# Up units of a SwiGLU block with seven half-block products in place of eight

## The reference

```
x = layer_norm(ALPHA * x + m @ lw['w_o'], lw['ln1_g'], lw['ln1_b'])
gate, up = jnp.split(x @ lw['w_up'], 2, axis=-1)          # w_up: 1024 x 5632
x = layer_norm(ALPHA * x + (jax.nn.silu(gate) * up) @ lw['w_down'], lw['ln2_g'], lw['ln2_b'])
```

## Time and profile before

| what | value |
|---|---|
| median of three executions | 2097.69 us |
| span of the profiled execution, first to last instruction | 2097.1 us |
| TensorE, matmul busy | 2072.3 us (99%) |
| VectorE busy | 1169.4 us (56%) |
| ScalarE busy | 713.2 us (34%) |
| GpSimd busy | 81.3 us (4%) |
| matmuls | 16020 |

### The profile page before, as it was taken

How to read it: one execution, slowest core, us unless ns; L and a number is a source line. 1 busy time by engine, 2 the same in 40 slices (tenths; PEclk the granted TensorE clock), 3 DMA queues, 4 the chain that set the end, 5 groups by cost and what they waited for, 6 DMA issues and landing times.

```text
span 2097.1 us, 38539 instructions
## 1 busy us (share of the span) xinstructions
PE 2072.3 (99%) x16020; PEld 1996.6 (95%) x16020; DVE 1169.4 (56%) x1886; ACT 713.2 (34%) x1152; POOL 81.3 (4%) x96
## 2 busy tenths in 40 slices
PE   7999999999999999999999999999999999999999
PEld 6899999898999999999998999989889999999998
DVE  5434645774377666654465365466724866566433
ACT  4232134444343232222343221354433433222232
POOL 1000000000011000000010000010000200000110
PEclk9999999999999999999999999999999999999999
DMA  5232222321132223223333222132213223323331
GB/s 171 78 77 58 61 54 64 93 62 51 51 101 81 85 85 90 83 81 93 86 92 83 78 59 76 40 93 59 63 34 93 84 81 90 90 80 88 84 90 54
DMA packets 287876, 163.45 MB, mean 78 GB/s; under 512 B 8984, under 2 KB 279552, under 8 KB 287744
## 3 DMA queue, kind: packets, MB, share of 16 engines
q1 hardware_dynamic: 283712, 152.07, 25.9%
q0 software_dynamic: 3552, 8.36, 1.3%
q10 hardware_dynamic: 480, 1.13, 0.2%
HBM read 156.86 MB, written 4.66 MB: 77 GB/s over the span
## 4 chain that ended last, share of the span: by engine, by line
PE 97%; DVE 1%; ACT 1%; issue 0%; DMA 0%; DVEq 0%; ACTq 0%
PE acc L696 50%; PE acc L682 27%; PE ring L718 4%; PE ring L802 2%; PE ring L956 2%; PE ring L975 1%; PE acc L718 1%; PE ring L964 1%; PE ring L1026 1%; PE ring L1008 1%; PE ring L1256 1%; PE ring L853 0%; PE ring L839 0%; PE ring L829 0%; PE ring L832 0%; PE acc L845 0%
## 5 line engine op out<-in xcount | busy, mean ns | idle before, releaser
L1388 ACT ACTIVATE whi<-raw 128x1024 fp32r<-128x1024 f32 (+6 forms) x340 | 312.0, 918 | 739.2 <-PE acc L696 404.0
L1970 DVE TENSOR_TENSOR wlo<-raw,whi 128x1024 fp32r<-128x1024 f32 (+6 forms) x340 | 355.0, 1046 | 299.7 <-ACT whi L1388 298.8
L696 PE MATMUL acc<-xh,whi 128*128 128x272 f32 x1376 | 310.7, 307 | 3.6 <-DVE xl L1970 3.4
L682 PE MATMUL acc<-xh,whi 128*128 128x274 f32 x1472 | 308.5, 290 | 0.0
L682 PE MATMUL acc<-xh,wlo 128*128 128x274 f32 x1472 | 305.9, 289 | 0.0
L682 PE MATMUL acc<-xl,whi 128*128 128x274 f32 x1472 | 305.5, 289 | 0.0
L696 PE MATMUL acc<-xh,wlo 128*128 128x272 f32 x1376 | 285.9, 289 | 0.0
L696 PE MATMUL acc<-xl,whi 128*128 128x272 f32 x1376 | 285.7, 289 | 0.0
L696 PEld LDWEIGHTS acc<-xh,whi 128*128 128x128 f32 x1376 | 218.2, 190 | 19.1 <-issue 14.4
L682 PEld LDWEIGHTS acc<-xh,whi 128*128 128x128 f32 x1472 | 232.2, 189 | 0.6
L682 PEld LDWEIGHTS acc<-xl,whi 128*128 128x128 f32 x1472 | 231.6, 189 | 0.0
(11 more groups left out here) (411 smaller groups left out, 3118.2 us busy)
## 6 DMA issues: line engine op xcount, KB each, us to landing
raw<-in_w_in_dram SPq DMA_DIRECT2D x104, 512.0 KB, 3.7
raw<-in_w_up_dram SPq DMA_DIRECT2D x88, 512.0 KB, 3.7
raw<-in_w_down_dram SPq DMA_DIRECT2D x32, 512.0 KB, 3.8
raw<-in_w_o_dram SPq DMA_DIRECT2D x16, 512.0 KB, 3.8
raw<-in_w_down_dram SPq DMA_DIRECT2D x16, 384.0 KB, 3.3
...
```

The lines of the kernel that those rows point to most:

```text
L682: last = pe.matmul(dst[:, at_:at_ + x1 - x0], wq[:, k * P:(k + 1) * P], x[:, k, x0:x1], start=k == 0 and q == 0, stop=k == KD - 1 and q == 2)
L696: last = pe.matmul(dst[:, b * 512:b * 512 + HALF], w[:, c:c + P], x[:, k0 + a, b * HALF:(b + 1) * HALF], start=start and a == 0 and q == 0 ...
L1388: return act.activation(dst, src, ACT.Copy)
L1970: return dve.tensor_tensor(out, a, b, op)
```

## The change

For the hidden blocks f = 4 to 21 (18 of 22, named **pairs**, p = 0 to 17), the product of x (two halves of the tokens by two halves of the depth) with the weights of both units (two halves of the depth by gate and up) is formed as a 2x2 by 2x2 block product with seven block products in place of eight, by the scheme of Strassen and Winograd. One block product is 4 k-blocks x 3 passes x 272 columns: 12 matmuls. Before, the same block took 8 k-blocks x 3 passes x 2 halves x 2 units = 96 matmuls; now it takes 84.

- **Activations.** The scheme takes x normalised. VectorE's `x_norm` and ScalarE's `x_gained` now do this within the first eight units, and VectorE makes four sums of blocks of x (`block_sums`, 128x1088 each). The seven blocks are split into high and low parts (`block_hi`, `block_lo`). `times_rstd` and `less_mean` leave the down stage; ScalarE only multiplies by ALPHA there.
- **Weights.** For each pair GpSimd makes four sums of quarters of the weights in three instructions (`weight_sum`: one 128x1024, two 128x512). Seven blocks of 128x512 are split by ScalarE (`weight_hi`) and VectorE (`weight_lo`), six products ahead of TensorE, into eight slots that reuse `whi`, `wlo`, and the space of `xh`/`xl`.
- **Results.** Products 0, 2, 4 and 6 of a pair add up in one bank of PSUM, 1 and 5 in a second, 3 in a third. Four intermediate values are copied out by ScalarE (`keep`), before TensorE adds the next product to the same bank. VectorE joins them (`pair_lin`), ScalarE takes the sigmoid, VectorE multiplies (`pair_h`).
- **Hidden values.** They stay unsplit in `hid` until the last pair, where ScalarE and VectorE split all 22 blocks, two at a time (`h_hi`, `h_lo`, 128x1088 each, 11 of each).
- The hardware loops of the up stage are gone; all is written out.

The diff, cut to what the prediction speaks of:

```diff
+STD_F = 4
+PAIRS = KF - STD_F
+SLOTS, AHEAD = 8, 6
+U_PAIRS = U_UP + 2 * STD_F
+
+PRODUCTS = ("x11_w11", "s3_t3", "s2_t2", "x12_w21", "s1_t1", "x22_t4", "s4_w22")
+OF_PAIR = len(PRODUCTS)
...
+                if 0 <= p < PAIRS:
+                    sp.wait_ge(*at("wt_lo", l, OF_PAIR * (p + 1)))
+                    passed(sp, "sp")
+                return not 0 <= p < PAIRS
...
+            for i, dst in enumerate((a, b, a, c, a, b, a)):
+                q = OF_PAIR * p + i
+                pe.wait_ge(*at("wt_lo", layer, q + 1))
+                if p == 0:
+                    pe.wait_ge(*at("xb_lo", layer, i + 1))
+                if p > 1 and i == 0:
+                    pe.wait_ge(*at("pr_h", layer, 2 * (p - 2) + 1))
+                elif p > 1 and i == 1:
+                    pe.wait_ge(*at("pr_lin", layer, 3 * (p - 2) + 3))
+                elif p > 1 and i == 3:
+                    pe.wait_ge(*at("pr_lin", layer, 3 * (p - 2) + 1))
+                elif i in (2, 4, 5, 6):
+                    pe.wait_ge(*at("pr_kept", layer, 4 * p + {2: 1, 4: 3, 5: 2, 6: 4}[i]))
+                w1, w2 = weight_slot(q)
+                first = i in (0, 1, 3)
+                for k in range(4):
+                    for r, (w, part) in enumerate(((w1, 0), (w1, 1), (w2, 0))):
+                        last = pe.matmul(dst[:, 0:HALF], w[:, k * P:(k + 1) * P], block_of(i, part)[:, k, :],
+                                         start=first and k == 0 and r == 0, stop=k == 3 and r == 2, skip_group_check=True)
+                last.then_inc(*inc("pr_done"))
...
+            if name in WEIGHT_TERMS:
+                act.wait_ge(*at("wt_sum", l, 3 * p + WEIGHT_TERMS[name]))
+            else:
+                loaded(l, U_PAIRS + 2 * p + (i == OF_PAIR - 1))
+            if q < SLOTS:
+                act.wait_ge(*used_unit(l, U_PAIRS - 2 if q < 2 else U_PAIRS - 1))
+            else:
+                act.wait_ge(*at("pr_done", l, q - SLOTS + 1))
+            copy(weight_slot(q)[0], weight_block(q)).then_inc(*inc("wt_hi"))
...
+            i = (0, 1, 2, 4)[n]
+            act.wait_ge(*at("pr_done", l, OF_PAIR * p + i + 1))
+            if p > 0:
+                act.wait_ge(*at("pr_lin", l, 3 * (p - 1) + (1, 2, 3, 2)[n]))
+            banks = pair_banks(p)
+            copy(kept[n], banks[1 if n == 1 else 0][:, 0:HALF]).then_inc(*inc("pr_kept"))
...
+            tail = {1: [(h_hi, 0), (h_hi, 2)], 2: [(h_hi, 4), (next_hi, U_DN)], 3: [(h_hi, 6)], 4: [(h_hi, 8), (h_hi, 10), (next_hi, U_DN + 1)],
+                    5: [(h_hi, 12)], 6: [(h_hi, 14), (h_hi, 16), (h_hi, 18), (h_hi, 20)]}
+            for p in range(PAIRS):
+                for i in range(OF_PAIR):
+                    if i in (0, 1, 2, 4):
+                        keep(l, p, (0, 1, 2, 4).index(i))
+                    if p == 0 and i == 0:
+                        act.sem_inc(*inc_by("w_hi", 2 * PAIRS))
+                        act.sem_inc(*inc_by("w_used", 2 * PAIRS))
+                    q = OF_PAIR * p + i + AHEAD
+                    if q < OF_PAIR * PAIRS:
+                        weight_hi(l, q)
...
+            def x_norm(l, k):
+                tt(y[:, k:k + 2, :], y[:, k:k + 2, :], rs[:, :].unsqueeze(1).broadcast_to([P, 2, T]), ALU.mult).then_inc(inc("x_prod", 2)[0], 2)
+                dve.wait_ge(*at("x_prod", l, k + 2))
+                tt(y[:, k:k + 2, :], y[:, k:k + 2, :], tmp[:, :].unsqueeze(1).broadcast_to([P, 2, T]), ALU.add).then_inc(inc("x_norm", 2)[0], 2)
...
+            def weight_lo(l, q):
+                dve.wait_ge(*at("wt_hi", l, q + 1))
+                hi, lo = weight_slot(q)
+                tt(lo, weight_block(q), f32(hi), ALU.subtract).then_inc(*inc("wt_lo"))
...
+                dve.wait_ge(*at("pr_sig", l, p + 1))
+                tt(gs[:, 0, :], gs[:, 0, :], gs[:, 1, :], ALU.mult).then_inc(*inc("pr_gate"))
+                dve.wait_ge(*at("pr_gate", l, p + 1))
+                dve.wait_ge(*at("pr_done", l, OF_PAIR * (p + 1)))
+                tt(hid[:, f, 0:HALF], gs[:, 0, 0:HALF], pair_banks(p)[0][:, 0:HALF], ALU.mult).then_inc(*inc("pr_h"))
+                tt(hid[:, f, HALF:T], gs[:, 0, HALF:T], hid[:, f, HALF:T], ALU.mult).then_inc(*inc("pr_h"))
...
+            x_steps = {1: [(x_norm, 0), (x_norm, 2)], 2: [(x_norm, 4)], 3: [(x_norm, 6)], 4: [(block_sums, B_S3), (block_sums, B_S1)],
+                       5: [(block_sums, B_S2), (block_sums, B_S4), (block_lo, 0)], 6: [(block_lo, 1), (block_lo, 2)],
+                       7: [(block_lo, 3), (block_lo, 4)]}
...
+            for q in range(2, AHEAD):
+                weight_lo(l, q)
+                if q < 4:
+                    block_lo(l, q + 3)
+            dve.sem_inc(*inc_by("w_lo", 2 * PAIRS))
+            tail = {1: [(h_lo, 0), (h_lo, 2)], 2: [(h_lo, 4)], 3: [(next_lo, U_DN), (h_lo, 6)], 4: [(h_lo, 8), (h_lo, 10)],
+                    5: [(h_lo, 12), (next_lo, U_DN + 1)], 6: [(h_lo, 14), (h_lo, 16), (h_lo, 18), (h_lo, 20)]}
+            for p in range(PAIRS):
+                for i in range(OF_PAIR):
+                    if i in (3, 4, 5):
+                        pair_lin(l, p, i - 3)
+                    if i == 6:
+                        pair_h(l, p)
+                    q = OF_PAIR * p + i + AHEAD
+                    if q < OF_PAIR * PAIRS:
+                        weight_lo(l, q)
+                    else:
+                        for step, n in tail[i]:
+                            step(l, n)
...
+                    pool.wait_ge(*at("wt_lo", l, OF_PAIR * p - 1))
+                pool.tensor_tensor(two(t13), later, earlier, ALU.subtract).then_inc(*inc("wt_sum"))
+            elif n == 1:
+                pool.wait_ge(*at("wt_sum", l, 3 * p + 1))
+                pool.tensor_tensor(t2, t13[:, 512:1024], w11, ALU.add).then_inc(*inc("wt_sum"))
+            else:
+                pool.wait_ge(*at("wt_sum", l, 3 * p + 2))
+                pool.tensor_tensor(t4, w21, t2, ALU.subtract).then_inc(*inc("wt_sum"))
```

283 lines of the change are left out of this document (211 added, 72 removed).

## The result

The changed kernel takes 2104.57 us (median of seven runs, 2100.29 to 2108.72), the kernel before 2097.69 us (seven runs, 2095.34 to 2098.98). The ratio is 1.0035, with an interval of 1.0025 to 1.0046: slower by a third of a per cent. I had forecast 2093 us. The time lies in the range of 2073 to 2110, but on the other side of no change, and above the 2084 to 2101 of my own case.

The account below looks back on a forecast made before the run. TensorE's matmuls were taken to bound the kernel. Per layer 28.8 - 14.1 - 4.8 - 7.6 = 2.3 us gained, 4.6 in all: span 2097.1 becomes 2092.5, forecast 2093 us, range 2073 to 2110 (8 in 10).

Parts of the forecast that it names:

- my own case: Whole kernel: the gain on TensorE is nearly eaten, 2084 to 2101 us; chance 0.52.
- first product of the pairs: Entry: VectorE's list from its copy after unit 1 takes 46.1 us, so TensorE starts the pairs 9.8 late.
- from there to product 6 of pair 0: Entry: low blocks and GpSimd's sums delay the first pair; 13.5 us against 10.3 plus 1.3.
- sixteen pairs: Up stage: sixteen pairs paced by VectorE, counted at 10.85 us each against TensorE's 10.55; 4.8 us lost a layer.
- from there to the first down matmul: Exit: VectorE's last splits and products delay the first down unit; 7.6 us lost a layer.
- rest of the layer, beside before: Down stage: VectorE loses 16 steps but was idle half the time, so worth nothing.
- the pair in the steady state: Up stage: VectorE needs 10.9 us a pair against TensorE's 10.55, counted as 10.85; 4.8 us lost a layer.
- the slower rival: Pairs: GpSimd's turns cost more, a pair takes 11.3 us, total 2108; it decides from 11.0; chance 0.25.
- VectorE's own work: Steady pair: VectorE's splits, joins, gate and products 6.7 us, plus 0.2 for two dependent steps.
- the turns: Steady pair: GpSimd's three sums and VectorE exclude each other, costing VectorE 4.1 us a pair.
- waiting: Steady pair: VectorE waits about 0.3 us for the sigmoid.
- a wait of 7.2 us ahead of the down stage: Exit: the first down unit starts 7.2 us after the end of the last pair's product 6.

Follow-up runs that it names:

- e3: Changed kernel plus 48 unused matmuls in TensorE's wait between the last pair and the down stage; 2098.46 us.
- e2: Changed kernel with the three weight sums of each pair made by VectorE in place of GpSimd; 2080.83 us.
- e1: Changed kernel with GpSimd's sums made for the first two pairs only, later pairs reusing those of pair 1; 2090.19 us.
- e4: Changed kernel with the first down tile no longer waiting for the last pair's products, only the second; 2090.64 us.
- e10: As e8, with pair 0's sums moved to unit 9 and its first two weight splits behind unit 10's work; 2056.35 us.
- e8: Changed kernel with sums on VectorE, the first down tile's wait removed, hidden splits reordered, six plain blocks for four, preparation over twelve units; 2065.83 us.

## Why the prediction was wrong

Per layer, from the origin, in us:

| step | predicted | measured |
|---|---|---|
| first product of the pairs | 46.1 | 46.9 |
| from there to product 6 of pair 0 | 13.5 | 13.5 |
| sixteen pairs | 173.6 | 176.0 |
| from there to the first down matmul | 19.7 | 19.7 |
| rest of the layer, beside before | 0 | 1.7 and 2.0 later |

**The failed step** is the pair in the steady state, "Counting 10.85: 0.3 x 16 pairs = 4.8". A pair took 11.00, which is the very point from which I had let the slower rival decide. The terms were: VectorE's own work 6.9, measured 6.8; the turns 4.1, less 0.36 for the operation from PSUM that runs beside them, measured 4.24 less 0.35; waiting 0.3, measured 0.35. They add up to 10.94, and I wrote 10.9 and then counted 10.85. So 0.09 of the 0.15 was my own rounding. The rest is the balance of three terms: the turns 0.14 too low, the waiting 0.05 too low, VectorE's own work 0.1 too high. That I had taken 4.1, "near the measured 1.11 for 544", was the wrong choice among values that were close together: in proportion 1.11 gives 4.18. The Trainium skill ("GPSIMD Engine Reference", section "Elementwise — side-by-side cycle accounting") gave 4.26 by my estimate, which the 4.24 bears out. On a bound engine an error of 1.4% in a pair is 2.4 us a layer, 4.8 in all, while the whole gain forecast was 4.6.

**The missing term** is TensorE's clock. I forecast a wait of 7.2 us ahead of the down stage, and it came, 7.07 us. I priced it at its length only. The half clock behind it cost 4.0 us over two layers by the first 180 down matmuls of after and e3 (the medians differ by 6.1, see e3). With the wait filled the kernel is at 2098.46, which is no difference from before; with it, it is slower. The kernel before has no such wait in these stages, at a granted clock of 1.00, so that no row of them could show it. But the wait itself I had forecast, and the trace of before has the half clock elsewhere: 0.86 over 330 to 355, and 0.94 over 1355 to 1385. The Trainium skill ("TensorE: Matmul & The Clock Gate", section "HAM oscillation — how this bites in real kernels") describes it: waits between groups of matmuls bring the half rate back each time. The trace agrees for the waits of 4.5 to 7.4 us here; of those about 1.9 us some are followed by it and some are not (last section).

**Small ones.** The entry was 0.8 late. I had also read it as one wait of 10 us behind unit 7; 3.6 of the waiting came in the plain units, where GpSimd's sums held VectorE up (e2, without them, waits once, for 7.44). VectorE is the bound of the entry, so its sum, 46.1, was not changed by that. TensorE's matmul of 272 columns takes 0.1261 in the pairs, not 0.1256, so the gain was 28.1, not 28.8; VectorE being the bound, that did not count. Nor did the profiled execution of before stand 0.6 below the median. In every result that has both, an execution's time is 1.8 to 1.9 above its span; so that execution took 2098.9 us, 1.2 above the median.

In sum the span was 10.1 us above the forecast's 2092.5: 4.8 for the pairs, 1.6 for the entry, 0.6 for roundings in the up stage, 3.7 behind the first down matmuls, less 0.6 since this execution reached its first up stage earlier. The 3.7 are mostly the clock. From the first down matmul on, the first 180 are 2.1 and 2.3 us longer than before; the rest of the down stage gives back 0.5 and 0.4 (109.5 us for 110.0 in layer 1).

**What held.** The count of the matmuls; that VectorE and GpSimd take turns and only the operation from PSUM is spared (the rule of "SBUF — State Buffer", section "Who interferes with whom", in the Trainium skill; the rows of the pairs show the same pattern throughout); that the wait in a pair shows before product 6 at ScalarE's copy; GpSimd busy 5.96 us a pair; the length of the entry and of the exit; no wait for a load. The mechanism of the slower rival, a higher price of the turns, decided on the pairs, but with 11.0 and not its 11.3; what took it from no difference to slower was the clock, which was in no case of mine. That the time still lies in the range of 2073 to 2110 owes something to its width: none of its cases has this cause.

Of the causes, the price of the sums in the steady state is shown by e1 and e2, the clock by e3, the exit by e4. That the entry costs what it does is shown less directly, by e10 with e8. Why the rest of the down stage takes 0.5 us less than before is open; VectorE's 16 steps fewer there may be the reason, but that was not tried. Open, too, is what sets the length of the half clock in the stage of small matmuls, which moves layer 1 by up to 4 us between these kernels.
